# Start of a decoder-layer kernel: the first weight tile and the first blocks of x asked for in another order, and the units of work sorted by new landing times

## What is computed

```python
def rmsnorm(x, g):
    xf = x.astype(jnp.float32)
    y = xf * lax.rsqrt(jnp.mean(xf * xf, axis=-1, keepdims=True) + EPS)
    return (y * g.astype(jnp.float32)).astype(x.dtype)

def swiglu(h, w1, w3, w2):
    return (jax.nn.silu(h @ w1) * (h @ w3)) @ w2
...
    x = x + 0.5 * swiglu(rmsnorm(x, ffn1_norm[l]), ffn1_w1[l], ffn1_w3[l], ffn1_w2[l])
```

## Time and profile before

| | |
|---|---|
| median of 3 runs | 1708.27 us (1708.21 to 1708.96) |
| the profiled execution | 1707.91 us |
| its span, slowest core (core 4) | 1706.0 us |
| spans of the eight cores | 1702.1 to 1706.0 us |
| granted TensorE clock, mean of each core | 0.998 to 0.999 |
| TensorE busy | 1663.0 us, 97% |
| VectorE, ScalarE, GpSimd busy | 931.0, 685.9, 322.6 us |
| DMA traffic | 142.65 MB, mean 84 GB/s |

### The profile page before, as it was taken

One profiled execution on the slowest core, in us unless ns is written; L12 is line 12 of the kernel. 1 busy time (PEld: TensorE's weight loads), 2 busy tenths in 40 slices (PEclk: granted clock), 3 DMA queues, 4 the chain that ended last, 5 costly groups with the idle time before them and its releaser, 6 DMA issues.

```text
span 1706.0 us, 23838 instructions; the slowest of 8 cores (1702.1 to 1706.0 us)
## 1 busy us (share of the span) xinstructions
PE 1663.0 (97%) x8060; PEld 797.7 (47%) x8218; DVE 931.0 (55%) x1513; ACT 685.9 (40%) x1074; POOL 322.6 (19%) x341
## 2 busy tenths in 40 slices
PE   5999999999999999999999999999999999999997
PEld 3544445455444544444545444444444444444444
DVE  4678453223579776556676433668753222423456
ACT  4531111112247768676777733445330111011144
POOL 1111002011002554434335453100000000000000
PEclk9999999999999999999999999999999999999999
DMA  8944476155584322313201773752331222220022
GB/s 169 197 66 78 120 149 94 26 87 102 148 193 112 65 42 58 64 38 58 61 22 38 186 149 111 184 131 49 52 50 25 50 38 34 41 38 13 7 99 99
DMA packets 77621, 142.65 MB, mean 84 GB/s; under 512 B 22592, under 2 KB 45120, under 8 KB 72768
## 3 DMA queue, kind: packets, MB, share of 16 engines
q0 software_dynamic: 25344, 62.40, 24.3%
q1 hardware_dynamic: 52160, 78.73, 15.1%
HBM read 165.74 MB, written 33.55 MB: 117 GB/s over the span
## 4 chain that ended last, share of the span: by engine, by line
PE 91%; DVE 3%; DMA 2%; issue 2%; ACT 1%; POOL 0%; DVEq 0%; SPq 0%; ACTq 0%; POOLq 0%
PE bank L758 89%; DMA X<-x 1%; DMA W<-f_w 1%; DVE XC L1315 1%; PE bank L1482 0%; PE bank L1485 0%; DVE hT L995 0%; ACT MU L774 0%; DVE T L1393 0%; DVE T L1391 0%; DVE SG L1498 0%; PE bank L1514 0%; DVE SG L1406 0%; POOL ATP L1528 0%; DVE X L995 0%
## 5 line engine op out<-in xcount | busy, mean ns | idle before, releaser
L758 PE MATMUL bank<-hT,W 128*128 128x512 bf16 (+1 forms) x2857 | 615.9, 373 | 5.7 <-DVE hT L995 1.8
L758 PEld LDWEIGHTS bank<-hT,W 128*128 128x128 bf16 x2912 | 286.1, 98 | 324.9 <-issue 3.3
L774 ACT ACTIVATE STMP<-bank 128x512 f32<-128x512 f32 (+1 forms) x182 | 105.5, 582 | 538.7 <-PE bank L758 517.5
L758 PE MATMUL bank<-HID,W 128*128 128x512 bf16 (+1 forms) x1417 | 310.6, 373 | 2.6 <-DVE HID L1081 1.0
L1099 DVE SCALAR_TENSOR_TENSOR X<-bank,X 128x512 f32<-128x512 f32 (+1 forms) x264 | 176.7, 673 | 189.9 <-PE bank L758 189.4
L1081 DVE TENSOR_TENSOR HID<-bank,STMP 128x512 bf16<-128x512 f32 (+1 forms) x182 | 120.5, 671 | 247.9 <-PE bank L758 242.8
L758 PEld LDWEIGHTS bank<-HID,W 128*128 128x128 bf16 x1448 | 141.4, 98 | 161.4 <-issue 1.8
L788 POOL DMA_DIRECT2D W<-f_w x88 | 47.1, 547 | 739.2 <-PE bank L758 570.1
L774 ACT ACTIVATE SQN<-X 128x1024 bf16<-128x1024 f32 (+2 forms) x100 | 86.5, 883 | 132.6 <-DVE X L1099 57.2
L758 PE MATMUL bank<-hT,GW 128*128 128x512 bf16 x497 | 117.5, 379 | 2.9 <-DVE T L1393 2.1
L758 PE MATMUL bank<-hT,LW 128*128 128x512 bf16 x501 | 117.6, 379 | 0.9 <-DVE SG L1406 0.3
(11 more groups left out here) (161 smaller groups left out, 1755.9 us busy)
## 6 DMA issues: line engine op xcount, KB each, us to landing
W<-f_w POOLq DMA_DIRECT2D x44, 512.0 KB, 6.8
W<-f_w POOLq DMA_DIRECT2D x44, 256.0 KB, 9.3
park<-X SPq DMA_DIRECT2D x8, 1024.0 KB, 7.2
gate_scr<-GU SPq DMA_DIRECT2D x64, 128.0 KB, 1.9
GIN<-gate_scr SPq DMA_DIRECT2D x8, 1024.0 KB, 11.4
X<-park SPq DMA_DIRECT2D x8, 1024.0 KB, 14.5
X<-x SPq DMA_DIRECT2D x7, 1024.0 KB, 11.7
out<-X SPq DMA_DIRECT2D x12, 512.0 KB, 3.0
```

The costliest lines, as they stand in the source:

```text
L758: ins = e.matmul(out_ap, l, r, start=(start and i == 0), stop=(stop and i == n - 1), skip_group_check=skip)
L774: P.add("act", lambda e: e.activation(out, in_, func, **kw), reads=reads, writes=writes, cost=act_cost(n, nap), tab=tab)
```

## The change

The first weight tile waits for the constants instead of the first transfer of x. gcol is asked for right behind the first two transfers of x. The megabyte of q1 waits until the second transfer of q0 has landed; q2 waits for q1 and q3 for q2; each comes as two transfers of 512 KB issued together. W1 waits for W0 and W2 for W1, W3 for q2, W4 for W2, W5 for W3. The numbers by which the units are sorted are new: (W0, q0), (W1, q0), (W0, q1), (W1, q1), then W2. `MARGIN` goes from 200 to 300 ns and `LOOK` from 6 to 8, for the plan of the whole kernel.

```diff
--- before.py
+++ after.py
@@ -23,12 +23,12 @@
 LAT = {("pe", "act"): 480.0, ("pe", "dve"): 530.0, ("pe", "pool"): 900.0, ("pe", "sp"): 450.0, ("pe", "pe"): 0.0}
 LAT_TO = {"pe": 115.0, "act": 95.0, "dve": 103.0, "pool": 145.0, "sp": 80.0}
 OVL = {"pe": 0.0, "act": 46.0, "dve": 79.0, "pool": 31.0, "sp": 0.0}
-MARGIN = {"pe": 200.0}
+MARGIN = {"pe": 300.0}
 DMA_NS_PER_B = 1.0 / 285.0
 DMA_LAT = 2500.0
 TAB_NS = 1283.0
 TAB_HOLD = 0.0
-LOOK = 6
+LOOK = 8
 PASSES = 24
 
 SLACK = {"pe": 0.0, "act": 0.0, "dve": 0.0, "pool": 0.0, "sp": 0.0}
@@ -621,8 +621,8 @@
 NRAW = 0
 FULL = (2, 4)
 FLOOK = 1
-ARR_W = (3.0, 4.0, 6.0, 7.0, 9.0, 10.0)
-ARR_X = tuple(a + (0.5 if q < NRAW else 2.5) for q, a in enumerate((1.0, 2.0, 5.0, 8.0)))
+ARR_W = (9.3, 16.3, 23.2, 27.0, 31.0, 35.0)
+ARR_X = (10.0, 16.5, 23.7, 29.0)
 
 
 def build(stage=None):
@@ -1705,26 +1705,30 @@
     P.boost = 9.8e8
     xb = load_x(0, 4, 4, 0, 256)
     P.boost = 9.7e8
-    xq = [load_x(0, 0, 8, 256, 256)]
+    sp_dma(gcol.ap, gains_d, [], gcol.hs, 128 * 6 * KC * 4)
     P.boost = 9.6e8
-    sp_dma(gcol.ap, gains_d, [], gcol.hs, 128 * 6 * KC * 4)
-    wh = [f1.load13(xa)]
+    consts_early()
+    wh = [f1.load13(cst.hs)]
     P.boost = 9e8
-    consts_early()
     act(warm.ap[:, 0:1], cst.ap[:, 1:2], AF.Exp, cst.hs, warm.hs, 1, tab=S_EXP)
     P.boost = 7.9e8
-    wh.append(f1.load13(xq[0]))
+    load_x(0, 0, 4, 256, 256, xb)
+    xq = [load_x(0, 4, 4, 256, 256, xb)]
     P.boost = 7.8e8
-    xq.append(load_x(1, 0, 8, 0, 256, wh[0]))
+    wh.append(f1.load13(wh[0]))
     P.boost = 7.7e8
+    load_x(1, 0, 4, 0, 256, xq[0])
+    xq.append(load_x(1, 4, 4, 0, 256, xq[0]))
+    P.boost = 7.6e8
     wh.append(f1.load13(wh[1]))
-    P.boost = 7.6e8
+    P.boost = 7.5e8
+    load_x(1, 0, 4, 256, 256, xq[1])
+    xq.append(load_x(1, 4, 4, 256, 256, xq[1]))
+    P.boost = 7.4e8
     wh.append(f1.load13(xq[1]))
-    P.boost = 7.5e8
-    xq.append(load_x(1, 0, 8, 256, 256, wh[2]))
-    P.boost = 7.4e8
+    P.boost = 7.3e8
+    wh.append(f1.load13(wh[2]))
     wh.append(f1.load13(wh[3]))
-    wh.append(f1.load13(xq[2]))
     for i in range(6):
         f1.load2(wh[4] if i < 3 else wh[5])
     for hf in range(2):
```

## The result

| | before | after |
|---|---|---|
| median of 22 runs, us | 1708.38 | 1712.16 |
| ratio after/before | | 1.0016, 95% interval 1.0009 to 1.0023 |
| profiled execution, us | 1707.91 | 1712.61 |
| its spans, eight cores, us | 1702.1 to 1706.0 | 1702.7 to 1711.1 |

The change makes the kernel slower by 0.16%, 2.7 us by the ratio. Executions in which one half of the chip was slowed are left out of the ratio, while the medians hold them. The forecast was 1705.4, at most 1709.5.

What follows compares the result with a forecast made beforehand. PE, busy 97% of the span, was taken as the bound. The start's -2.3 us and the constants' -0.5 summed to -2.8, giving 1705.1 from the profiled execution and 1705.5 from the median; 1705.4 was taken, range 1702.2 to 1709.5.

Steps and rivals of the forecast that it cites:

- the first product: Start of the first FFN on PE: the first product comes at 17.0 instead of 19.31 us.
- the +0.9: Second block of x, beside the early W0: it lands 0.9 us later, at 9.7 rather than 8.8.
- gcol's wait: Before DVE's first hT: asking for the gains first removes a wait of 2.2 us.
- q1's products: First FFN: they start at 26.85 us, 9.85 after the first product, with two table loads in the chain.
- the second slow spell: Rival, at PE's gap before q1's products: PE falls to the lower pace, 2.1 us more, 1707.5; chance 0.20.
- Of the four later waits (3.6 us) 0.6 are left: PE's norm waits before the second FFN matrix: earlier x rounds leave 0.6 of 3.6 us.
- The rival of long rounds: Rival, x transfers: rounds take 10.0 us, so PE waits and slows, 6.9 us more, 1712.3; chance 0.09.
- 42.75: From q1's products to the second FFN matrix: 42.75 us of products, norm sums and waits, ending at 69.6.
- The engines may be the bound whichever transfer is asked first: Rival, first transfers: x eats gcol's gain and the change has no effect, 1708.3; chance 0.04.
- MARGIN and LOOK at -0.5: Re-plan, 250 to 1000 us: a larger margin removes some short PE waits, -0.5 us.
- bounds of -3.2: PE's waits from 250 to 1000 us: at most 3.2 us can be won, as much may be lost.
- the half taken: Waits of 0.2 to 0.3 us in 250 to 1000 us, 1.1 in all: half credited as won, -0.5.

Runs made afterwards that it cites:

- e10: The start alone with W4 asked for when W3 has landed and W5 when q3 has; ratio 1.0005 to the kernel before.
- the start alone: The change with MARGIN back at 200 and LOOK at 6, so only the new transfers and unit order; ratio 1.0007 to the kernel before.

## Why the prediction was wrong

**Right: the first product.** W0 was asked for at 3.00 (forecast 2.9), the second block of x was with ACT at 8.75 (9.7; W0 did not hold it up at all, the +0.9 was too careful), gcol's wait was gone, and the first product came at 15.99 (17.0), 15.3 to 16.9 over the cores.

**Right: q1.** Its round took 6.8 us (7.7), it landed at 14.9 to 16.1 (17.5), and the SiLU with its two table loads stood in the chain, row for row as forecast. From the first product to q1's took 10.3 us (9.85), and q1's products started at 26.29 (26.85). The wait for W1 on core 0, 1.93, was not forecast (landing 21.5, forecast 18) but fell into the gap.

**Right as a rival, not in the forecast: the second slow spell.** PE idled 2.70 us ahead of 26.29, and the first window below is at the lower of the clock's two levels, 1.2 GHz (granted 0.50); the second stands behind the wait of 2.96. Stretch, length, busy (count), clock, DMA share, GB/s:

```profile
26.29:28.38 2.09, 2.09 (x11) 0.50 1.01 196
42.55:43.80 1.25, 1.25 (x10) 0.79 0.91 295
```

The Trainium skill (TensorE: Matmul & The Clock Gate, section Part 1) has the engine start at the slow clock and fall back to it when idle; this trace agrees, with idle times of 2.70, 2.96 and 4.76 us on core 0, where the earlier trace rows had only one of 7. The spells cost core 0 4.3 us in all. But by the runs with unused products, removing most of them wins at most 0.3 us of time, since a transfer is what PE meets next.

**The step that failed** is "Of the four later waits (3.6 us) 0.6 are left, since the x rounds are asked for at 9.8, 17.6 and 25.5". The round of q2 fits (8.1 us, no wait). The last was asked for at 24.6, earlier than forecast, and took 15.56 us: the rest of W2, then W3, W4 and at the end W5 went with it. The flight had been priced with one tile beside it and was used for every round, though by the diff W3 and W4 are both under way in the last. The rival of long rounds had the mechanism, "a round longer than 8 us" and the wait returns, but put its 10 us at q1's round and its weight at 0.09. From q1's products to the second matrix core 0 took 49.1 us, forecast 42.75: 2.8 for waits (3.4 in place of 0.6), 2.6 for the lower pace behind q1's start, and 0.9 left, by which the count was short (core 4, with one wait of 0.26 and 1.3 at the lower pace, took 44.4). In the mean of the eight cores it was 46.9, with waits of 2.1 and about 2 at the lower pace. So the term of the waits and the lower pace, which the forecast put at nothing and left to a rival, weigh about the same; and e10, where the wait for q3 is gone, shows that the first doesn't come back as time by itself.

Behind it stands a larger omission. The earlier trace rows showed the DMA engines 93% and 76% busy while PE worked, and the chain of before was transfers to 41 us. All of x for two blocks must arrive before q3's sum, and the tiles that the products ahead of it need. What was there to win was the hole of the earlier trace rows, and it was filled, as the windows view of core 0 shows (DMA share 0.94, then GB/s):

```profile
13.50:16.80 3.30, 0.81 (x4) 0.59 (x5) 2.58 (x7) 1.90 (x4) 0.43 (x1) 1.00 0.94 178
```

The last round did not gain by it. Before, q3 landed at 35.0 to 38.1; after, at 36.2 to 40.6. Holding a tile back that is not needed yet does move it (32.4 to 35.3 in e10), so the bound is the engines together with what is put ahead of q3. "The engines may be the bound whichever transfer is asked first" was written down and given 0.04.

**The other term that failed** is MARGIN and LOOK at -0.5, between bounds of -3.2 and as much the other way. Measured +2.4 (0.14% alone, interval 0.05 to 0.23). The bounds held, the half taken did not: the wait that was to shrink did (2.1 to 1.1), and two others came. The changes of one constant, +0.44% to +0.65%, lie far outside the bounds. With 3.2 us of waits to win in 750 us and no row that limits what a new order can lose, a forecast of zero with a range mostly on the slow side would have fitted better.

**The metric.** The forecast was for one core, core 4, and that core met it (69.67) by luck: its first products and q1's came 1.5 us earlier than forecast, and the stretch behind took 1.6 us longer (44.4 in place of 42.75). Its last round, 13.0 us, was mis-sized as well, but q3 landed at 36.2 and was wanted at 38.3. The other seven arrive at 71.3 to 75.4. Before, the spread at the second matrix was 68.5 to 71.9. One might blame the new chain, in which each x waits for the x before. The spans say otherwise: the cores are no further apart with that chain alone (3.0 us in the start alone, 3.9 before), but they are with the new constants (6.6). Why an order of PE should spread the cores is not shown.

## What to carry to other kernels

Before crediting an earlier first product, follow the chain of waits to the last transfer that the stage needs and ask whether that one lands earlier; if the DMA engines are 90% busy all the way, only a hole in them can be won, or what is asked for too early can be held back. Price each transfer's flight by the requests that travel with it, the last ones too. A constant that re-plans a whole kernel is a draw from the waits of a new order, on the slowest core: try several values, and expect a loss where the order at hand has few waits. A difference of 1 us between single profiled executions is worth nothing until the spans of all the runs agree.

## What the runs showed of the hardware

With the change, a megabyte of x, asked for as two transfers of 512 KB, had landed 6.0 to 8.6 us after the second request, by core, in the rounds of q1 and q2 with one weight tile beside it at a time. It took 13.0 to 15.6 us in the round of q3, with W2, W3 and W4 on their way. In that round, on core 0, x had none of the engines in one stretch, 39.9% in another and 9.3% in a third.

The first transfer of x, asked for 1.06 us after each core's own first instruction, landed either at 4.7 to 5.4 us or at 6.7 to 8.1. In each of the 18 profiled executions it was exactly one core of every pair (0 and 1, 2 and 3, 4 and 5, 6 and 7) that was late, and which one changed from execution to execution: the two cores of a pair do not get equal service in the first 10 us. Whether that is carried on depends on the kernel: at the second matrix the late cores are at 72.9 and the others at 73.1 with the change, but at 73.1 and 70.7 in the start alone.
